# A two-layer decoder: the ends of both attention parts, last rows' norm on other engines, levels taken later

## The reference

```
h = h + mixer(rmsnorm(h))              # layer 0: mLSTM and gated linear attention; layer 1: windowed attention
u = rmsnorm(h) * ffn_norm[layer]
group = argmax(u @ wg + bg)            # one of 4 groups
top2  = the two best of the group's 8 experts by u @ we + be
h = h + sum of gate * expert(u) over the two    # expert: silu(u @ w_gate) * (u @ w_up) @ w_down
```

## Time and profile before

| what | us |
|---|---|
| median of 3 runs (lowest to highest) | 2071.75 (2071.66 to 2072.22) |
| span of the profiled execution | 2068.1 |
| median less span | 3.65 |
| TensorE busy | 2005.8 |
| VectorE busy | 1576.0 |
| ScalarE busy | 1338.0 |
| GpSimd busy | 277.5 |

### The profile page before, as it was taken

How to read it: one execution, slowest core, us unless ns; L and a number is a source line. 1 busy time by engine, 2 the same in 40 slices (tenths; PEclk the granted TensorE clock), 3 DMA queues, 4 the chain that set the end, 5 groups by cost and what they waited for, 6 DMA issues and landing times. The chain is left out here.

```text
span 2068.1 us, 29817 instructions
## 1 busy us (share of the span) xinstructions
PE 2005.8 (97%) x10448; PEld 1636.6 (79%) x10448; DVE 1576.0 (76%) x1878; ACT 1338.0 (65%) x1818; POOL 277.5 (13%) x345
## 2 busy tenths in 40 slices
PE   7999998998999999999998989999899999999998
PEld 6888876887788888888886866777688888888885
DVE  4561235776888898889888357887898988889886
ACT  5332425663787878887873157664688777878784
POOL 2000000001211111111103422110211111112210
PEclk9999999999999999999999999999999999999999
DMA  4112222124999999999996020013799999999996
GB/s 142 41 58 86 71 75 88 72 75 179 350 384 390 388 389 386 382 376 383 387 358 214 1 78 25 22 62 113 267 390 385 383 385 387 387 387 386 383 356 258
DMA packets 123487, 513.24 MB, mean 248 GB/s; under 512 B 27373, under 2 KB 28490, under 8 KB 89610
## 3 DMA queue, kind: packets, MB, share of 16 engines
q1 hardware_dynamic: 103674, 474.11, 61.0%
q0 software_dynamic: 18576, 33.86, 4.3%
q10 hardware_dynamic: 1152, 4.19, 0.5%
HBM read 495.05 MB, written 50.86 MB: 264 GB/s over the span
## 5 line engine op out<-in xcount | busy, mean ns | idle before, releaser
L517 DVE TENSOR_TENSOR exp_w_lo<-ring_raw,first_w_hi 128x2048 fp32r<-128x2048 f32 x192 | 438.8, 2287 | 32.7 <-ACT first_w_hi L444 32.6
L517 DVE TENSOR_TENSOR exp_w_lo<-ring_raw,exp_w_hi 128x2048 fp32r<-128x2048 f32 x192 | 439.3, 2290 | 27.8 <-ACT exp_w_hi L444 27.7
L444 ACT ACTIVATE exp_w_hi<-ring_raw 128x2048 fp32r<-128x2048 f32 x192 | 367.8, 1918 | 60.4 <-PE exp_up_out L369 32.5
L444 ACT ACTIVATE first_w_hi<-ring_raw 128x2048 fp32r<-128x2048 f32 x188 | 360.5, 1918 | 60.9 <-PE exp_up_out L369 30.1
L314 POOL DMA_INDIRECT y_rows<-exp_y,base_rows_y x63 | 79.0, 1254 | 947.2 <-ACT exp_y L464 934.0
L369 PE MATMUL exp_gate_out<-exp_w_lo,exp_x_hi 128*128 128x512 f32 x512 | 199.8, 390 | 0.0
L369 PE MATMUL exp_y_out<-exp_w_lo,exp_hid_hi 128*128 128x512 f32 x512 | 199.6, 390 | 0.0
L369 PE MATMUL exp_up_out<-exp_w_lo,exp_x_hi 128*128 128x512 f32 x512 | 199.2, 389 | 0.0
L369 PE MATMUL exp_gate_out<-first_w_hi,exp_x_hi 128*128 128x512 f32 x272 | 109.3, 402 | 3.1 <-issue 2.0
L521 DVE TENSOR_TENSOR exp_x_lo<-exp_x_turned,exp_x_hi 128x1024 fp32r<-128x1024 f32 x62 | 75.9, 1224 | 47.6 <-ACT exp_x_hi L448 47.6
L369 PEld LDWEIGHTS exp_up_out<-exp_w_lo,exp_x_hi 128*128 128x128 f32 x512 | 96.1, 188 | 19.8
(11 more groups left out here) (535 smaller groups left out, 4632.2 us busy)
## 6 DMA issues: line engine op xcount, KB each, us to landing
ring_raw<-in_expert_w_gate_dram SPq DMA_DIRECT2D x128, 1024.0 KB, 10.9
ring_raw<-in_expert_w_up_dram SPq DMA_DIRECT2D x128, 1024.0 KB, 11.4
ring_raw<-in_expert_w_down_dram SPq DMA_DIRECT2D x128, 1024.0 KB, 11.3
l0w_raw<-in_ab_w_in_dram SPq DMA_DIRECT2D x48, 256.0 KB, 2.8
finish_y<-y_rows SPq DMA_DIRECT2D x8, 1024.0 KB, 12.7
ring_raw<-in_swa_w_qkv_dram SPq DMA_DIRECT2D x5, 1024.0 KB, 9.4
ring_raw<-y_rows SPq DMA_DIRECT2D x10, 512.0 KB, 4.4
base_h<-in_x_dram ACTq DMA_DIRECT2D x8, 512.0 KB, 6.8
```

Source lines behind the costliest of these rows:

```text
L444: nc.scalar.activation(split[split_slot(unit)][0][:], raw[raw_slot(unit)][:], ACT.Copy).then_inc(hi_ready, 1)
L517: nc.vector.tensor_tensor(lo[:], raw[raw_slot(unit)][:], hi[:].bitcast(F32), ALU.subtract).then_inc(lo_ready[split_slot(unit)], 1)
```

## The change

In both layers:

- `norm_last_rows` is removed from VectorE's stream. GpSimd multiplies the second half of each chunk of the last rows by the gain, as soon as both halves of `h[:, T - 1]` are written, ahead of its two memsets. ScalarE's `scale_last_rows` then scales all 1024 columns. The store waits for that alone.
- ScalarE squares the last row tile in halves. The first half, with its share of the mean and eps, is done once `residual(b, 0)` is written. The router's columns are copied before the root is taken.
- `take_levels` is split. The maximum (`take_most`) stays; the other three operations move behind the barriers, to the head of VectorE's part of the experts. Every engine waits for a new semaphore `leveled` before it loads the number of levels.

In layer 1 alone: 6 spare turns before `turn_rows(b, 1)`, 4 between the halves of `route_product(b)`, and 20 instead of 24 before `rank(b)`.

The diff, without declarations and with parts alike shown once:

```diff
@@ take_levels
-def take_levels(v, dve, c, R, counted):
-
+def take_most(v, R, counted):
     v.tensor_reduce(R.most, counted, AX.X, ALU.max)
-    dve.drain()
+
+
+def take_levels(v, dve, c, R):
+
     v.tensor_scalar(R.full, c["limits"][:, 1:], R.most, None, ALU.is_lt)
     dve.drain()
     v.tensor_reduce(R.filled, R.full, AX.X, ALU.add)
     dve.drain()
-    v.tensor_copy(R.levels[:], R.filled[0:1, :])
+    return v.tensor_copy(R.levels[:], R.filled[0:1, :])
@@ experts_over
         def each_block(engine, body, first=None, last=None):
 
+            engine.wait_ge(s["leveled"], 1)
             count = engine.value_load(R.levels[0:1, 0:1], min_val=0, max_val=LEVELS - 1)
...
         def vector(dve):
+            take_levels(nc.vector, dve, c, R).then_inc(s["leveled"], 1)
+
             def body(b, e):
@@ layer0, sync (layer 1 the same)
-                    sp.wait_ge(s["r_rows_made"], t + 1)
-                    if t + 1 == T:
+                    if t + 1 < T:
+                        sp.wait_ge(s["r_rows_made"], t + 1)
+                    else:
                         sp.wait_ge(s["last_rows_scaled"], 1)
@@ layer0, gpsimd
+                by_chunk = lambda x: x.rearrange("p (q k) -> p k q", k=8)
+                pool.wait_ge(s["gain_ready"], 16)
+                pool.wait_ge(stored[T % SLOTS], 32)
+                pool.wait_ge(s["h_made"], 2 * T)
+                g.tensor_tensor(chunks(slots[:, T % SLOTS])[:, :, 64:P], by_chunk(h[:, T - 1])[:, :, 64:P], by_chunk(gain_row[:])[:, :, 64:P], ALU.mult)\
+                    .then_inc(s["last_gained"], 1)
                 pool.wait_ge(s["o_made"], 2 * T)
                 g.memset(ahead.x_rows[0][:], 0.0)
@@ layer0, scalar
+                def h_root_last():
+                    u, junk = T - 1, slots[:, (T - 1) % SLOTS]
+                    for half in range(2):
+                        cols = slice(half * BANK, (half + 1) * BANK)
+                        act.wait_ge(s["h_made"], 2 * u + half + 1)
+                        a.activation(junk[:, cols], h[:, u, cols], ACT.Square, accum_out=c["half_sum"][:, 0:1] if half == 0 else c["sums"][:, u:u + 1])
+                        act.drain()
+                        if half == 0:
+                            a.activation(c["half_sum"][:, 1:2], c["half_sum"][:, 0:1], ACT.Identity, bias=c["eps"][:], scale=1.0 / 1024)
+                    router_cols(u, 1)
+                    a.activation(root[:, u:u + 1], c["sums"][:, u:u + 1], ACT.Sqrt, bias=c["half_sum"][:, 1:2], scale=1.0 / 1024).then_inc(s["h_rooted"], 1)
+
                 def scale_last_rows():
-                    rows_b = chunks(slots[:, T % SLOTS])[:, :, 0:64]
-                    act.wait_ge(s["last_gained"], 1)
+                    rows_b = slots[:, T % SLOTS]
+                    act.wait_ge(s["last_gained"], 2)
                     act.wait_ge(s["last_scaled"], 1)
                     a.activation(rows_b, rows_b, ACT.Copy, scale=scale[:, T - 1:T]).then_inc(s["last_rows_scaled"], 1)
...
-                h_root(T - 1)
-                router_cols(T - 1, 1)
+                h_root_last()
                 scale_last_rows()
@@ layer0, vector
-                def norm_last_rows():
-                    v.scalar_tensor_tensor(last_rows[:, :, 64:P], by_chunk(h[:, T - 1])[:, :, 64:P], scale[:, T - 1:T], by_chunk(gain_row[:])[:, :, 64:P],
-                                           ALU.mult, ALU.mult).then_inc(s["r_rows_made"], 1)
...
                 take_logits(b, -1, -1)
-                norm_last_rows()
                 ranks_of(b)
                 mark(b)
                 entries_of(a)
                 dve.wait_ge(s["counted"], 1)
-                take_levels(v, dve, c, R, counted)
+                take_most(v, R, counted)
+                dve.drain()
                 entries_of(b)
@@ layer1, gpsimd
+            pool.wait_ge(s["gain_ready"], 16)
+            pool.wait_ge(s["h_made"], 2 * T)
+            g.tensor_tensor(chunks(r_rows[T - 1])[:, :, 64:P], by_chunk(h[:, T - 1])[:, :, 64:P], by_chunk(row_a[:, 0:1024])[:, :, 64:P], ALU.mult)\
+                .then_inc(s["last_gained"], 1)
             pool.wait_ge(s["o_made"], 2 * T)
             g.memset(ahead.x_rows[0][:], 0.0)
@@ layer1, tensor
+            def spare_turns(n):
+                for k in range(n):
+                    nc.tensor.transpose(wide[1][:, 2 * BANK + (k % 4) * P:2 * BANK + (k % 4 + 1) * P], c["ident"][:], c["ident"][:])
+
...
                 project_out(b, 1, 6, 8)
+                spare_turns(6)
                 turn_rows(b, 1)
                 rank(a)
                 route_product(b, range(4))
+                spare_turns(4)
                 route_product(b, range(4, 8))
                 enter(a)
-                idle_turns(24)
+                idle_turns(20)
                 rank(b)
```

More of the change, by code:

```diff
@@ L100, in __init__ @@
         small = mem.sb("choice", [P, 8])
-        self.most, self.filled = small[:, 0:1], small[:, 1:2]
+        self.most, self.filled, self.full = small[:, 0:1], small[:, 1:2], mem.sb("full", [P, 8])[:]
     def scratch(self, x, exact, y):
@@ L108, in scratch @@
         self.made, self.masked = y[:, 0:256], y[:, 256:288]
-        self.group_top, self.full = y[:, 288:296], y[:, 318:326]
+        self.group_top = y[:, 288:296]
         self.group_at, self.chosen_at = y[:, 296:304].bitcast(U32), y[:, 304:312].bitcast(U32)
@@ L657, in experts_over @@
         hid_turned, y_out = mem.ps("hid_turned", [P, 4, P]), mem.ps("y_out", [P, 1024])
-        names = ("weights", "gathered", "x_turned_", "x_cols_", "multiplied", "silued", "hid_", "hid_turned_", "hid_cols_", "y_made", "y_copied", "scattered", "stored", "ended")
+        names = ("weights", "gathered", "x_turned_", "x_cols_", "multiplied", "silued", "hid_", "hid_turned_", "hid_cols_", "y_made", "y_copied", "scattered", "stored", "ended", "leveled")
         s = {n: mem.sem(n) for n in names}
         def each_block(engine, body, first=None, last=None):
+            engine.wait_ge(s["leveled"], 1)
             count = engine.value_load(R.levels[0:1, 0:1], min_val=0, max_val=LEVELS - 1)
@@ L2863, in router_cols, with last_square @@
                 a.activation(r_cols[:, 4 * half:4 * half + 4], four(row_bank(u, half)), ACT.Copy).then_inc(s["r_cols_made"], 1)
+            def last_square(half):
+                u, cols = T - 1, slice(half * BANK, (half + 1) * BANK)
+                act.wait_ge(s["h_made"], 2 * u + half + 1)
+                a.activation(work[0][:, cols], h[:, u, cols], ACT.Square, accum_out=c["half_sum"][:, 0:1] if half == 0 else c["sums"][:, u:u + 1])
+                act.drain()
             def scale_last_rows():
-                rows_b = chunks(r_rows[T - 1])[:, :, 0:64]
-                act.wait_ge(s["last_gained"], 1)
+                rows_b = r_rows[T - 1]
+                act.wait_ge(s["last_gained"], 2)
                 act.wait_ge(s["h_scaled"], T)
@@ L2912, in scalar @@
                 router_cols(u, 0)
-                h_squares(u)
-                act.drain()
-                a.activation(root[:, u:u + 1], c["sums"][:, u:u + 1], ACT.Sqrt, bias=c["eps"][:], scale=1.0 / 1024).then_inc(s["h_rooted"], 1)
-                router_cols(u, 1)
+                if u + 1 < T:
+                    h_squares(u)
+                    act.drain()
+                    a.activation(root[:, u:u + 1], c["sums"][:, u:u + 1], ACT.Sqrt, bias=c["eps"][:], scale=1.0 / 1024).then_inc(s["h_rooted"], 1)
+                    router_cols(u, 1)
+                else:
+                    last_square(0)
+                    a.activation(c["half_sum"][:, 1:2], c["half_sum"][:, 0:1], ACT.Identity, bias=c["eps"][:], scale=1.0 / 1024)
+                    last_square(1)
+                    router_cols(u, 1)
+                    a.activation(root[:, u:u + 1], c["sums"][:, u:u + 1], ACT.Sqrt, bias=c["half_sum"][:, 1:2], scale=1.0 / 1024).then_inc(s["h_rooted"], 1)
             scale_last_rows()
@@ L3051, in gain_last_rows @@
                     .then_inc(s["last_gained"], 1)
-            def norm_last_rows():
-                v.scalar_tensor_tensor(chunks(r_rows[T - 1])[:, :, 64:P], by_chunk(h[:, T - 1])[:, :, 64:P], scale[:, T - 1:T], by_chunk(row_a[:, 0:1024])[:, :, 64:P],
-                                       ALU.mult, ALU.mult).then_inc(s["r_rows_made"], 1)
             def take_logits(u, t_ranked, t_entered):
```

4 lines of the change are left out of this document (2 added, 2 removed).

## The result

The changed kernel takes 2081.39 us (median of 5 runs, 2080.6 to 2083.1), the kernel before on the same chip 2072.22 (5 runs, 2071.66 to 2072.7). Forecast were 2070.8 us and a range up to 2073.0, so the time lies 8.4 us outside it. The span of the profiled execution grew from 2068.1 to 2080.7 us, by 12.6 us, TensorE's busy time from 2005.8 to 2014.4 us.

The account below looks back on a forecast made before the run. TensorE, busy throughout the experts, was taken as the bound, so only the two handovers from attention to experts count: +0.6 us in layer 0 and -1.6 in layer 1 give -1.0, from 2071.75 to 2070.8 us; range 2069.0 to 2073.0.

Parts of the forecast that it names:

- the multiply on GpSimd: Behind the last residual: takes 1.8 us (bounds 1.26 and 2.5) and holds VectorE's L153 to its end in layer 0.
- So the marks are late by 498.97 - 497.97 = 1.0 us: Layer 0's handover: L153, held by GpSimd's multiply, delays VectorE's marks by 1.0 us (0.45 if short, 1.7 if long).
- 0.2 at most, taken as 0: Layer 1's handover: delay of L153 by GpSimd's multiply, which is over at 1436.1 (0.7 us if it takes 2.5).
- +0.6 and -1.6 us: Forecast change of the handovers up to the gathered rows' turning: layer 0 longer by 0.6 us, layer 1 shorter by 1.6.
- VectorE's marks are late next: Layer 0's handover: after 0.11 us gained by the halved square, GpSimd's multiply makes the marks 1.0 us late.
- B: the multiply is long (2.5 us) and holds VectorE in both layers: Rival, chance 0.12: layer 0 +1.3 us, layer 1 -0.9, total 2072.1 us.
- I think that it holds: Layer 1's tail: TensorE's clock stays at 2.4 GHz, 20 turns take 2.4 us instead of 5.32, ranks 2.5 us sooner.
- I take it that the clock falls here too: Layer 1's head: clock at 0.50 behind a 3.6 us pause, so first turn to turned rows takes 4.07 us.
- The levels: Moved to the experts' heads: +0.6 us in layer 0, 0.65 in layer 1; the 0.61 saved in layer 0's tail stays hidden.
- VectorE's norm gone: Between choosing and ranks: removing norm_last_rows gains 0.52 us in layer 0 and lets layer 1's 2.5 us out.
- The square in halves: Ahead of VectorE's logits: ScalarE's earlier first half gains 0.11 us in layer 0 and 0 in layer 1.

Follow-up runs that it names:

- e3: The changed kernel with GpSimd's two memsets waiting until VectorE has marked the last tile, the multiply left in place: 2078.13 us (10 runs), ratio 1.0019.
- p2: The changed kernel with GpSimd's multiply replaced by five memsets of the same 512 columns, each behind a drain: 2072.27 us (one run; kernel before 2073.65).
- e8: The changed kernel with GpSimd's multiply and memsets waiting for the marks of the tile before the last: 2076.37 us (one run; kernel before 2073.65).
- p1: The changed kernel with the gain multiplied in plain column order on GpSimd and VectorE, instead of steps of eight: 2077.75 us (one run).
- e9: The changed kernel with idle turns (26 in layer 0, 20 in layer 1) in TensorE's pause ahead of the marks: 2080.12 us (4 runs), ratio 1.0043.
- e6: The kernel before with only the square in halves and layer 1's moved turns (6, 4, then 20 instead of 24): 2072.61 us (10 runs), ratio 1.0007.
- e1: The changed kernel without GpSimd's multiply, the last rows' second half normed by VectorE again: 2073.02 us (10 runs), ratio 1.0003.
- e7: e6 plus, in layer 1, VectorE multiplying the second half by the gain right behind the last residual, norm_last_rows gone there: 2073.52 us (10 runs), ratio 1.0011.
- e5: The kernel before with only the levels moved to the experts' head: 2074.96 us (10 runs), ratio 1.0012.

## Why the prediction was wrong

**The step that failed** is the multiply on GpSimd: "So the marks are late by 498.97 - 497.97 = 1.0 us" in layer 0 and "0.2 at most, taken as 0" in layer 1. Measured behind the last residual, the marks reach TensorE 3.09 us later than without this part in layer 0 (6.39 against 3.30) and 1.86 later in layer 1 (6.12 against 4.26). Of the whole handover, last residual to rows turned, +0.6 and -1.6 us were forecast and +5.34 and +2.23 measured. Three things were off in the step.

*The duration.* 2.32 us instead of 1.8, inside the bounds of 1.26 to 2.5; in layer 1 it is 2.06. It also starts 0.87 us behind the residual's start, where 0.7 was taken. L153 was held as worked out, to the multiply's end: 1.68 us more in layer 0 (1.90 against 0.22) and 0.43 in layer 1 (0.65 against 0.22).

*What stands behind it on GpSimd.* I asked what waits behind the held instruction on VectorE and didn't ask what is queued behind the multiply on GpSimd. Two memsets are, and they push L155 to 1.64 and 1.65 us, from 0.17 without them. With L153 that is 1.68 + 1.47 = 3.15 us in layer 0 and 0.43 + 1.48 = 1.91 in layer 1, within 0.1 us of the 3.09 and 1.86 above. e3 takes the second term away and gives 1.41 us of it back in both layers.

*Which instructions are held.* I looked only for VectorE instructions with two SBUF operands, as L3004 was the earlier trace rows. L155, L162 and L120 have one, and memsets hold them (p2, e8) while they leave L153 alone; L120 was held by the multiply too (e8, layer 1). L162 in the trace before, 1.32 us beside a memset, would have shown it. The Trainium skill, "SBUF — State Buffer", section "Who interferes with whom", says both: that a VectorE instruction with two SBUF inputs contends only with a GpSimd that reads, and that tensor_scalar can enter a two-port mode, in which it contends with GpSimd. I cited the first half in the prediction; p1, p2 and e8 agree with both (0.22 us for L153 beside a memset, 1.65 for L155).

**What follows from it.** "VectorE's marks are late next" and "B: the multiply is long (2.5 us) and holds VectorE in both layers" had the kind of the loss, at 2072.1 us, and not its size. In layer 0 TensorE's wait for the marks is 3.14 us, the clock is at 0.50 from 501.82, inside it, and the 24 turns behind it take 5.19 us; so TensorE, not the norm, is what the ranks wait for (chosen to ranks 2.80 us, where 503.76 - 503.09 = 0.67 was reckoned). Where the clock holds (e9, layer 1 of e3), it is 0.67 us. A fall in the first expert and one in layer 1's attention come on top, which the range allowed a margin for and the sum did not.

**Layer 1.** "I think that it holds" is right for the turns alone: e6 has 1.00 there, 2.35 us for the 20 turns and 1.98 us sooner ranks, where 2.5 less the norm were forecast. In the changed kernel the held marks leave a pause of 2.40 us, the clock falls at 1450.73, the 20 turns take 3.70 us, and the ranks at 10.44 us are no sooner than before (10.37). "I take it that the clock falls here too" came true: 0.50 over 6.82 us from 1460.97.

**The other terms.** The levels cost +0.62 and +0.76 us at the heads (forecast +0.6 and +0.65) and win nothing in the tail, as forecast. VectorE's norm gone is worth 0.52 to 0.55 us between choosing and ranks (1.19 to 1.22 down to 0.67; forecast 0.52). The square in halves can't be read from the runs: where nothing holds L153, layer 0's marks come at 3.29 to 3.80 us with it (e1, e6, e7, e8, p2) and at 3.69 and 3.97 without (before, e5), a spread above the forecast's 0.11. Part of the spread is the second memset, which holds L162 or not by the moment at which it starts: in e5 and e6 the marks are done 3.92 and 3.74 us behind the residual, in e8, where nothing holds them, 3.23. The kernel e1, with the levels, the turns and the halves together, stands at 1.0003 [0.9994, 1.0013]: about 1 us either way can't be told from nothing.

**Still open.** The time of an execution moves with TensorE's clock: the kernel before ranges over 7.3 us in 25 runs on one chip, and the four with a mean clock of 0.996 took 2070.59 to 2070.92 us, the one with 0.991 took 2077.51. But the mean clock alone doesn't give the loss: e9's two runs at 0.995 took 2079.50 and 2079.64 us, the kernel before's four at 0.995 took 2070.76 to 2072.15. Which falls a change causes and which it merely meets isn't settled by one profile of each, and it is why e6's 1.98 us and e9's 2.2 us are shown in the handover and not in the total. Nor do the runs tell where the 0.025 us for each expert comes from, nor all of the 6 us by which e9's stretch between the experts and the residual is longer than before. No kernel here beats the one before.

## What to carry to other kernels

Work that moves to an idle engine moves the whole queue behind it too: list what GpSimd does next, then look up, instruction by instruction, what VectorE does in all of that time. In these runs VectorE's operations on two SBUF operands waited for the end of a GpSimd multiply, which reads SBUF, and its operations with one SBUF operand and a scalar (TENSOR_SCALAR) waited beside the multiply and beside memsets, with as few as 2 columns. A trace of the kernel as it is can show such a hold already: look for small instructions that take far longer in one place than elsewhere. Where such a tail is the handover to an engine that is never idle, half a microsecond that VectorE saves isn't worth four on GpSimd.

## What the hardware showed that was not expected

An instruction on 128x2 elements took 1.64 us (L155) instead of 0.17, as it was held across two memsets that follow each other. It isn't always so: with a drain between memsets it was let in after the current one (0.47 us), but L167 was let in behind the first of two without a drain (1.00 us, e3), and L120 was held across the multiply and both memsets in layer 0 of e8 (2.69 us) and to the end of the multiply alone in layer 1 (0.86 us). What decides this is open. A GpSimd multiply of 128x512 took 1.27 us in plain order and 2.32 with operands and result in steps of eight, 2.06 with the other layer's buffers; L153 ended 0.08 us after it in both layers of the changed kernel.
